# Two hybrid blocks in one float32 kernel: the delta rule's steps in another order, and norms worked by halves

## The reference, cut to what matters

```python
f = swiglu(rms_norm(h, ffn1_pre_g[l]), ffn1_w_gate[l], ffn1_w_up[l], ffn1_w_down[l])
h = h + FFN_RESIDUAL_SCALE * rms_norm(f, ffn1_post_g[l])
u = rms_norm(h, mix_pre_g[l])
...                                   # four mixers of u @ w_in, gated and merged
h = h + rms_norm(merged @ w_o[l], mix_post_g[l])
f = swiglu(rms_norm(h, ffn2_pre_g[l]), ffn2_w_gate[l], ffn2_w_up[l], ffn2_w_down[l])
h = h + FFN_RESIDUAL_SCALE * rms_norm(f, ffn2_post_g[l])
```

```python
qkv_b = jax.nn.silu(causal_depthwise_conv_2(qkv_b, conv_w))       # four taps
qb, kb, vb = jnp.split(qkv_b, (QK_B, 2 * QK_B), axis=-1)
qb, kb = l2norm(qb), l2norm(kb)
decay = jnp.exp(jnp.where(causal, g[..., :, None] - g[..., None, :], NEG_INF))
lower = jnp.where(strict, (kb * beta) @ kb.T * decay, 0.0)
t_inv = inverse(lower + eye)
...                                   # values and states through t_inv
o = o * rsqrt(mean(o * o) + eps) * dn_norm_g * silu(z)
yb = o @ w_branch_b
```

## Time and profile before

| | us |
|---|---|
| median of 3 runs | 3259.92 (3257.59 to 3264.05) |
| the profiled execution, its own time | 3261.25 |
| its span in the trace | 3259.6 |
| PE busy, PEld busy | 3045.4 (93%), 2883.8 (88%) |
| DVE busy | 1881.4 (58%) |
| ACT busy | 1340.2 (41%) |
| POOL busy | 524.2 (16%) |
| granted TensorE clock, mean | 0.966 |

### The profile page before, as it was taken

How to read it: one execution, slowest core, us unless ns; L and a number is a source line. 1 busy time by engine, 2 the same in 40 slices (tenths; PEclk the granted TensorE clock), 3 DMA queues, 4 the chain that set the end, 5 groups by cost and what they waited for, 6 DMA issues and landing times.

```text
span 3259.6 us, 59469 instructions
## 1 busy us (share of the span) xinstructions
PE 3045.4 (93%) x22178; PEld 2883.8 (88%) x22178; DVE 1881.4 (58%) x3364; ACT 1340.2 (41%) x2214; POOL 524.2 (16%) x791
## 2 busy tenths in 40 slices
PE   8999999999999999998898988999989998899998
PEld 7989998998989999897798878989989897899897
DVE  4556876555555876555455467455555546653555
ACT  4344454434334454433334544434333355443332
POOL 0000000000000000000003555440000055456000
PEclk9999999999999999999998999999999999999999
DMA  5544445454554445455663222254546522123453
GB/s 205 186 161 150 140 146 182 165 185 159 185 180 148 140 146 171 166 190 156 191 215 128 95 78 79 79 181 162 202 146 222 178 96 99 66 79 135 164 196 130
DMA packets 72445, 495.51 MB, mean 152 GB/s; under 512 B 8064, under 2 KB 8240, under 8 KB 20176
## 3 DMA queue, kind: packets, MB, share of 16 engines
q1 hardware_dynamic: 67824, 471.95, 42.2%
q0 software_dynamic: 4048, 18.59, 2.1%
q10 hardware_dynamic: 272, 0.99, 0.1%
HBM read 487.31 MB, written 4.19 MB: 151 GB/s over the span
## 4 chain that ended last, share of the span: by engine, by line
issue 71%; PE 16%; POOL 5%; DVE 4%; DVEq 1%; ACT 1%; POOLq 1%; DMA 1%; ACTq 0%; SPq 0%
PE psum L1153 5%; POOL weights_low L942 4%; PE psum L1065 4%; PE psum L1122 1%; PE psum L1263 1%; POOL small L898 1%; DMA weight_ring<-stream 1%; PE psum L1490 1%; DVE work L2260 1%; POOLq L897 1%; PE psum L1367 1%; PE psum L1209 1%; PE psum L1488 0%; PE psum L1478 0%; ACT weights_high L1558 0%
## 5 line engine op out<-in xcount | busy, mean ns | idle before, releaser
L1558 ACT ACTIVATE weights_high<-weight_ring 128x2048 fp32r<-128x2048 f32 (+5 forms) x778 | 906.0, 1184 | 1121.1 <-DMA weight_ring<-stream 1113.9
L1881 DVE TENSOR_TENSOR weights_low<-weight_ring,weights_high 128x2048 fp32r<-128x2048 f32 (+4 forms) x538 | 888.1, 1658 | 789.7 <-ACT weights_high L1558 786.8
L1065 PE MATMUL psum<-normed_t_high,weights_high 128*128 128x256 f32 x2816 | 801.4, 285 | 11.3 <-DVE normed_t_low L1890 9.9
L1065 PE MATMUL psum<-normed_t_low,weights_high 128*128 128x256 f32 x2816 | 798.9, 284 | 0.0
L1065 PE MATMUL psum<-normed_t_high,weights_low 128*128 128x256 f32 x2816 | 798.6, 284 | 0.0
L1065 PEld LDWEIGHTS psum<-normed_t_high,weights_high 128*128 128x128 f32 x2816 | 541.7, 192 | 17.7 <-DVE normed_t_low L1890 12.3
L1065 PEld LDWEIGHTS psum<-normed_t_low,weights_high 128*128 128x128 f32 x2816 | 542.4, 193 | 3.2
L1065 PEld LDWEIGHTS psum<-normed_t_high,weights_low 128*128 128x128 f32 x2816 | 542.1, 193 | 0.0
L1122 PE MATMUL psum<-weights_high,work_parts 128*128 128x512 f32 x1472 | 464.1, 397 | 13.5 <-DVE work_parts L1890 13.5
L942 POOL TENSOR_TENSOR weights_low<-weight_ring,weights_high 128x256 fp32r<-128x256 f32 x560 | 410.6, 765 | 223.3 <-ACT weights_high L1558 223.3
L1153 PE MATMUL psum<-normed_t_high,weights_high 128*128 128x256 f32 x1248 | 392.1, 314 | 2.8 <-DVE normed_t_low L1890 2.1
(11 more groups left out here) (267 smaller groups left out, 4347.0 us busy)
## 6 DMA issues: line engine op xcount, KB each, us to landing
weight_ring<-stream SPq DMA_DIRECT2D x400, 1024.0 KB, 4.9
weight_ring<-stream SPq DMA_DIRECT2D x64, 768.0 KB, 4.2
feature_rows<-feat POOLq DMA_DIRECT2D x6, 1024.0 KB, 7.6
work<-toeplitz_rows POOLq DMA_DIRECT2D x8, 512.0 KB, 6.5
feature_rows<-feat POOLq DMA_DIRECT2D x6, 512.0 KB, 4.1
toeplitz_rows<-work POOLq DMA_DIRECT2D x1, 3072.0 KB, 36.6
params<-prms POOLq DMA_DIRECT2D x5, 251.5 KB, 3.6
residual<-x SPq DMA_DIRECT2D x2, 512.0 KB, 4.8
```

What stands on the lines that cost most here:

```text
L1065: ins = pe.matmul(PS[:, bank, at:at + S], w[a][:, first + k, c * P:(c + 1) * P], src[b][:, k, :], start=(k, m) == (0, 0), stop=(k, m) == ( ...
L1558: return act.activation(dst, src, ACT.Copy, scale=scale)
L1881: dve.tensor_tensor(some(LOW, i, q, n), some(RING, i, q, n), some(HIGH, i, q, n).bitcast(F32), ALU.subtract).then_inc(low_by_vector, n)
```

## The change

It has two halves.

In the delta rule, `prepare` puts both heads' `ddc` ahead of everything else. In the first pair `dtr` of h0 comes ahead of the last turn of the attention, both `ddc` behind it, and the weights that tell how much of the dense work stands behind each step are set anew. `ACT`'s throw-away squares of `dtr` go to a tile that holds nothing at that time. The list of taps is no longer emptied between the pairs: it goes on into the next `solve`, is held back until the tiles it writes are free, and is emptied when a host needs its bank or a `(hp, None)` mark is met. A gate or `pz` unit is now the first of `extra`, ahead of the convolutions. `dot` leaves `solve`: it now follows three and five steps into the next pair's solve, in bank 3; for the last pair it stands behind eight rounds of the first gate of branch 1.

At the borders, `post` and `norm` of the first block square by halves of 512 columns, POOL adds two sums for a root (`rsqrt_of_halves`), DVE multiplies the sums by the gain while the root is still made (`gained`) and then adds by halves (`added`). `norm` writes H times root times gain as XN on DVE, with the gain as a row read from `feature_rows`, and TensorE turns it by transposes in place of the products with the diagonal. The two blocks' `xt` go by tokens: a bank holds four feature blocks of one tile. The first product waits for the banks of both tiles (first and third), and from its fifth block on for the others. `post2` scales by halves. A row DMA for the first gain is added at the start on POOL.

```diff
     def norm_in(s):
         pl.step("norm", ("norm", s), s=s,
-                signals=[("squares_summed", 2), ("rsqrt_ready", 2), ("normed_ready", 2)])
+                signals=[("squares_summed", 4), ("rsqrt_ready", 2), ("normed_ready", 4)])
...
+        for h in hs:
+            add(h, "ddc", [3], [("decay_ready", 1), ("strict_decay_ready", 1)])
         for h, b in zip(hs, banks):
             add(h, "dtr", b, [("qk_squares_summed", 1), ("qk_rsqrt_ready", 1)])
             add(h, "dte", [], [("head_scalars_ready", 1)])
         for h, b in zip(hs, banks):
-            add(h, "ddc", [3], [("decay_ready", 1), ("strict_decay_ready", 1)])
             add(h, "dtf", b)
...
-        both("dot", [("delta_out_ready", 1)])
         return steps
+
+    def dot(h):
+        pl.step("dot", ("dot", h), banks=[3], h=h, signals=[("delta_out_ready", 1)])
...
-    first = [(4, f) for f in prepare((0, 1), ((6, 7), (4, 5)))]
-    chain = steps + first[:1] + last + first[1:]
+    first = prepare((0, 1), ((6, 7), (4, 5)))
+    chain = steps + [(0, None), (3, first[2])] + last + [(2, f) for f in first[:2]]
+    chain += [(3, f) for f in first[3:5]] + [(9, first[5])] + [(4, f) for f in first[6:]]
...
-    interleave(pl, chain, dense)
+    later = interleave(pl, chain, dense, keep=True)
...
-            for n, item in enumerate(todo[:8]):
-                chain.insert(2 + 4 * n, item)
-            chain += todo[8:] + ends
-        interleave(pl, chain, extra[hp])
+            todo.insert(2, (hp + 1, None))
+            ends = chain[-2:]
+            chain = chain[:-2]
+            for n, item in enumerate(todo[:9]):
+                chain.insert(9 + 3 * n, item)
+            chain += todo[9:] + ends
+        later = interleave(pl, chain, extra[hp], later, keep=hp + 1 < pairs)
...
+            def rsqrt_of_halves(dst, halves, eps, signal, count):
+
+                for n in range(2):
+                    pool.wait_ge(squares_summed, reach("squares_summed", count + n))
+                    pool.tensor_tensor(dst, dst if n else EPSES[:, EPS_AT[eps], 0:1], halves[:, n:n + 1], ALU.add)
+                    pool.drain()
+                pool.tensor_tensor(dst, dst, HALFNEG[:, 0:1], ALU.pow).then_inc(signal, 1)
...
+                first = (named(("norm", st.s)).at["normed_ready"] if now.blk == 1 else 4 * st.s) - 3
+                for n, job in enumerate(st.jobs):
+                    t, half = n // 2, n % 2
+                    pe.wait_ge(bank_taken[job.bank], turn_at(job))
+                    pe.wait_ge(normed_ready, reach("normed_ready", first + n))
+                    for kk in range(4):
+                        k = 4 * half + kk
+                        ins = pe.transpose(PS[:, job.bank, kk * P:(kk + 1) * P], XN[:, t, k * P:(k + 1) * P], IDENT)
+                    ins.then_inc(bank_full[job.bank], 1)
...
-                    if fresh is not None and k % 2 == 0:
-                        ready = named(("xt", fresh)).jobs[k // 2]
-                        pe.wait_ge(bank_taken[ready.bank], taken_at(ready))
+                    if fresh is not None and k % 4 == 0:
+                        for t in range(T):
+                            ready = named(("xt", fresh)).jobs[2 * t + k // 4]
+                            pe.wait_ge(bank_taken[ready.bank], taken_at(ready))
...
             def norm(st):
+                dve.wait_ge(feature_rows_loaded, reach("feature_rows_loaded", 16 * st.s))
                 for t in range(T):
                     dve.wait_ge(rsqrt_ready, reach("rsqrt_ready", st.at["rsqrt_ready"] - 1 + t))
-                    dve.tensor_scalar(DG[:, t, :], IDENT, RS[:, t:t + 1], None, ALU.mult).then_inc(normed_ready, 1)
+                    for n in range(2):
+                        cols = slice(n * HALF, (n + 1) * HALF)
+                        dve.scalar_tensor_tensor(out=XN[:, t, cols], in0=H[:, t, cols], scalar=RS[:, t:t + 1],
+                                                 in1=PG[:, 1, cols], op0=ALU.mult, op1=ALU.mult
+                                                 ).then_inc(normed_ready, 1)
...
+                gained(0, 0)
+                gained(0, 1)
+                gained(1, 0)
+                added(0)
+                gained(1, 1)
+                added(1)
```

223 lines of the change are left out of this document (117 added, 106 removed).

## The result

The changed kernel takes 3279.94 us (median of 5 runs, 3274.75 to 3280.27) against 3259.92 for the kernel before. The ratio is 1.0052, with a 95% interval of 1.0041 to 1.0062: slower by 0.5%. The prediction was 3242, its range 3212 to 3262, with 0.12 for slower. So both the sign and the range were wrong. The profiled execution's span is 3278.3 us, 18.7 more than before.

A forecast was written before the change was run, and what follows sets the result against it. PE, busy 3045.4 of 3259.6 us, was taken as the bound, so only its waits and half clock counted. 3261.25 - 26.2 (delta rule) + 8.0 (borders) = 3243.0, forecast 3242 after a 1.3 profiling offset; range 3212 to 3262.

The forecast's parts named there:

- The waits that go: Delta rule: PE's waits for ddc, taps, turns, gate and some in levels vanish, with clock regained; -25.5 us a layer.
- The gate for POOL: Second gate at the delta rule's end: POOL's low parts do not get ahead, so 2.5 us is given back.
- The waits that come: Delta rule: new PE waits at dlb or dla where solves meet, +9.9 us, and clock, +2.5; +12.4 a layer.
- the solves' starts: Where one pair's solve ends in the next's start: DVE's queue 10.7 us against PE's 7.4, 3.3 waited at three places.
- my own sign: Wrong in the main if the delta rule's PE waits, about 31 us a layer, do not fall by at least 8.
- Inner first-block borders: Four mid-layer borders: turns 2.5 us less, half clock behind them 1.9 lost; -0.6 each, -2.4 together.
- My reading of 32 products: First-block borders: 16 transposes replace 32 products, which took 6.01 us at 0.19 each; 2.5 us less.
- The head: Program start: multiplications ahead of low parts, a longer wait for subtractions and lost clock; +4.5 us.
- Second-block borders: First product waits for both tiles' banks: +0.5 us at each of four, +1.4 at the second layer's first; +3.4.
- C: Solves' starts: DVE's queue decides, each of six costs 8 us and halves the clock after; about 3280 us, chance 0.10.
- A: Delta rule: the waits only move, layers gain 6 us each (-12); 3256 us, chance 0.17.
- D: First-block borders: DVE operations with two SBUF inputs shut POOL out of the shared port; +8, 3250 us, chance 0.10.

The follow-up runs named there:

- the half: The kernel before with only the delta rule's part of the change, borders as before: 3257.05 us, ratio 0.9989 to the kernel before.
- the borders' half: The kernel before with only the borders' part of the change, delta rule as before: 3281.00 us, ratio 1.0066 to the kernel before.
- the filled delta rule's half: Delta rule's part alone, borders of before, plus unread identity products (34, 22, 22; 22, 13, 13) while TensorE awaits the norm: 3258.16 us, ratio 0.9996.

## Why the prediction was wrong, by its own steps

**The waits that go** (-25.5 a layer, of it 7.9 of clock): right as to the waits. Those for `ddc`, for the taps ahead of `dtr` and for the last turn are gone, and in the levels about 8 of the 11.3 where I took 4; the rest of these is the starts'. The gate for POOL waits 2.0 us, for 2.5 given back. The clock did not come back: it is at half for 19.3 us, where it was for 15.8.

**The waits that come** (+12.4 a layer): the step that failed. I looked for DVE's queue at the solves' starts and nowhere else, and put every other place at nothing. The starts came out near their price: behind `dl0`, whose wait I had booked as moved, PE waits 3.8 us (1.41 and 2.37) at two of the three and nothing at the third, 7.6 a layer for 9.9, and DVE's row lasts 11.2 us for my 10.7. What I put at nothing cost 15.0 us of waits a layer. The taps that were no longer run down ahead of `dtr` were held back to just ahead of the gates, which need their banks: 3.60 and 2.95 us, with 5.8 at half clock behind the first, so more than the 5.73 that I had booked as gone. And the same edit that cleared the levels put `prepare` close together at the solve's end: 3.5 us at `dtr` and 4.9 at `dtf`. By my own sign, waits that fall by less than 8 us in a layer, I was wrong in the main: they fell by 4. The runs show that the starts' 7.6 come from the order of the units (with the old order only `dl0`'s 1.2 and 1.5 are left, and the half is 11.3 us faster), and that the late `prepare` is worth more than it costs (9 us). No run takes away the waits ahead of the gates, so their cause is read from the trace, and none puts `ddc` back alone.

**Inner first-block borders** (-2.4): right in mechanism and near in size. The turns' 2.5 less was 2.1 to 2.3, and 1.4 at one border; the stretches behind them grew by 1.4 to 2.4, where I had 1.9. My reading of 32 products was wrong in words, since the runs show that 16 float32 matmuls are listed as 32 instructions; the time was read from the row and stands.

**The head** (+4.5, measured +9.6): the added row DMA was costed at nothing. POOL's first root comes 5.1 us later (19.93 for 14.81), and 3.3 of the head come back when most of the row leaves POOL's queue. Every instruction of a step counts, those on POOL's queue too, and this one stood in the diff.

**Second-block borders** (+3.4, measured +8.5): the wait for three banks in place of one was seen and sized too low. I took 0.5 at four of them and 1.4 at one for what is 0.7 to 1.4 and 3.1, and left out the dearer affine step and the buffer it shares. Without the turns by tokens the borders' half is 11.3 us faster, so that they cost more than scaling by halves brings.

**The rivals.** The measured time is C's 3280, but not by C. Its starts cost 3.8 us behind `dl0` twice a layer, not 10.5 three times, and all of the loss stands at borders that it had at +8: luck. A, the waits only move, was right for the delta rule as a whole, with -2.3 where it had -12. For D (the port), the changed kernel's POOL additions at the inner border took 0.19 to 0.42 us, where one had taken 0.83. Its powers, 0.55 us when alone, took up to 1.11 beside DVE operations with both inputs in SBUF, such as this one:

```profile
578.83 0.83 POOL L941 TENSOR_TENSOR small<-small 128x1 f32<-128x1 f32 x1
```

DVE waited 0.44 us for it. So D had a part, but a small one: those borders came out near the forecast without it.

## What to carry to other kernels

Work that is put off is not gone. Ask which bank or buffer it holds and who asks for that next, and price the wait there before booking the old one as saved; go through every place to which an edit moves work, not only the one that looks worst. Where units and leftovers are woven together, the unit that comes last decides whether the leftovers run beside it or stand ahead of the next chain. At a border bound by other engines, TensorE's idle time can be filled with products nobody reads, but only as long as the fill ends before its operand comes.

## What the runs showed of the hardware

- A broadcast DMA over 127 partitions on SP's queue was still moving at 35 us, at 24 to 29 GB/s wherever it ran alone; over 112 partitions it landed 6.4 us after its issue at 2.3.
- A drain of POOL between two additions ended when the last DMA on POOL's own queue had landed: POOL went on 0.2 to 0.3 us behind the landing at 14.6, 15.6, 16.0 and 19.3 us, in four kernels.
- Behind 16 transposes at half clock the product ran at 0.50 for 3.4 us or more; behind the same turns as 32 matmul instructions, with the same idle time ahead of them but 2.3 us longer, at 1.00. With TensorE kept busy ahead of them the transposes ran at 1.00, and the product behind them too at three of four borders.
- In the second block the fill left the clock behind the turns at half: PE waits 2.4 and 1.4 us between and behind its transposes there, at 1746 and 1749 us of the filled delta rule's half.
- A power on one column took 0.55 us on POOL alone and 0.83 to 1.11 beside DVE operations with both inputs in SBUF.
